# Token tile 3 last: samples and parameters ahead of it, parameter loads on two queues, an early ScalarE table load, and tile 3's squares on GpSimd

## What is computed

```
x = concat(x_prompt [512, 2048], x_sample [32, 2048])        # T = 544 tokens
xn = x * rsqrt(mean(x*x, axis=-1) + 1e-6) * norm_g           # RMSNorm over 2048
u  = xn @ ab_w_in                                            # first projection, 8 DeltaNet + 4 GLA heads
...                                                          # mixers, output projection, gate,
                                                             # second layer (SSD + RG-LRU), final norm
```

## Time and profile before

| what | value |
|---|---|
| median of 3 runs | 2451.35 us (2448.93 to 2452.26) |
| profiled execution, span from first to last instruction | 2447.1 us |
| median of the runs over that span | 4.25 us |
| TensorE busy | 2384.2 us, 97% |
| VectorE, ScalarE, GpSimd busy | 1280.8, 958.4, 373.5 us |
| mean granted TensorE clock | 0.993 |

### The profile page before, as it was taken

One profiled execution on the slowest core, in us unless ns is written; L12 is line 12 of the kernel. 1 busy time (PEld: TensorE's weight loads), 2 busy tenths in 40 slices (PEclk: granted clock), 3 DMA queues, 4 the chain that ended last, 5 costly groups with the idle time before them and its releaser, 6 DMA issues.

```text
span 2447.1 us, 50327 instructions
## 1 busy us (share of the span) xinstructions
PE 2384.2 (97%) x21567; PEld 2273.9 (93%) x21567; DVE 1280.8 (52%) x2387; ACT 958.4 (39%) x1547; POOL 373.5 (15%) x558
## 2 busy tenths in 40 slices
PE   7999999999999999999999999999999999999996
PEld 7998999988999999899999999988899999999996
DVE  6655656565654564622444465566656663243432
ACT  5523444323444344432332353443355553243332
POOL 3101101111101101111111212122212211111111
PEclk9999999999999999999999999999999999999998
DMA  9433333333344454552233343233323354223232
GB/s 232 115 103 107 116 98 116 108 90 106 108 121 117 136 152 122 194 161 87 87 97 109 110 114 92 70 89 87 86 80 103 95 190 127 87 83 96 79 88 76
DMA packets 375535, 271.16 MB, mean 111 GB/s; under 512 B 24419, under 2 KB 346733, under 8 KB 374800
## 3 DMA queue, kind: packets, MB, share of 16 engines
q1 hardware_dynamic: 341424, 172.53, 26.0%
q0 software_dynamic: 22080, 72.77, 9.3%
q10 hardware_dynamic: 11808, 22.63, 2.6%
HBM read 220.24 MB, written 48.37 MB: 110 GB/s over the span
## 4 chain that ended last, share of the span: by engine, by line
PE 86%; DVE 6%; ACT 5%; issue 2%; DMA 1%; POOL 0%; ACTq 0%; DVEq 0%; POOLq 0%
PE psd L582 71%; PE psw L605 2%; PE psw L604 2%; PE psw L632 1%; PE psw L682 1%; DVE arena L1967 1%; PE psw L660 1%; PE psw L668 1%; ACT w_hi L1136 1%; DVE w_lo L1683 1%; PE psw L674 0%; PE psw L646 0%; PE psw L654 0%; PE psw L971 0%; PE psw L1066 0%
## 5 line engine op out<-in xcount | busy, mean ns | idle before, releaser
L582 PE MATMUL psd<-xh,w_hi 128*128 128x272 f32 x5056 | 1098.3, 298 | 8.9 <-DVE w_lo L1683 5.3
L582 PE MATMUL psd<-xl,w_hi 128*128 128x272 f32 x5056 | 1048.4, 289 | 2.9 <-DVE xl L1745 2.1
L582 PE MATMUL psd<-xh,w_lo 128*128 128x272 f32 x5056 | 1045.2, 288 | 0.0
L582 PEld LDWEIGHTS psd<-xh,w_hi 128*128 128x128 f32 x5056 | 795.0, 189 | 60.0 <-issue 40.5
L582 PEld LDWEIGHTS psd<-xh,w_lo 128*128 128x128 f32 x5056 | 796.4, 189 | 0.0
L582 PEld LDWEIGHTS psd<-xl,w_hi 128*128 128x128 f32 x5056 | 792.2, 189 | 4.2 <-DVE xl L1745 3.1
L1683 DVE TENSOR_TENSOR w_lo<-w_raw,w_hi 128x512 fp32r<-128x512 f32 x632 | 433.7, 706 | 380.5 <-ACT w_hi L1136 379.4
L1136 ACT CAST w_hi<-w_raw 128x512 fp32r<-128x512 f32 x632 | 376.7, 616 | 573.2 <-PE psd L582 499.3
L2590 POOL TENSOR_TENSOR states<-states,extra 128x544 f32<-128x544 f32 x59 | 86.7, 1469 | 514.4 <-ACT extra L1191 514.3
L2377 DVE TENSOR_TENSOR extra<-psd,rstd 128x544 f32<-128x544 f32 x32 | 23.2, 724 | 156.0 <-PE psd L582 138.9
L2350 DVE TENSOR_TENSOR arena<-arena,psd 128x544 f32<-128x544 f32 x32 | 23.1, 721 | 136.7 <-PE psd L582 129.9
(11 more groups left out here) (514 smaller groups left out, 2376.9 us busy)
## 6 DMA issues: line engine op xcount, KB each, us to landing
w_raw<-in_ab_w_in_dram SPq DMA_DIRECT2D x224, 256.0 KB, 3.0
w_raw<-in_cd_w_in_dram SPq DMA_DIRECT2D x148, 256.0 KB, 3.0
w_raw<-in_ple_w_gate_dram SPq DMA_DIRECT2D x128, 256.0 KB, 3.1
w_raw<-in_ab_w_out_dram SPq DMA_DIRECT2D x64, 256.0 KB, 2.8
w_raw<-in_cd_w_out_dram SPq DMA_DIRECT2D x64, 256.0 KB, 2.8
uT_scratch<-mix ACTq DMA_DIRECT2D x53, 272.0 KB, 2.2
hT_scratch<-arena POOLq DMA_DIRECT2D x8, 1088.0 KB, 6.4
arena<-hT_scratch POOLq DMA_DIRECT2D x8, 1088.0 KB, 9.5
```

The costliest lines, as they stand in the source:

```text
L582: mm = pe.matmul(out[:, D0 + HALF * half:D0 + HALF * (half + 1)], w[:, r, k % QH, :], x[:, k, HALF * half:HALF * (half + 1)], start=(k == ...
```

## The change

The samples are loaded, transposed and copied between x1 and x2, and their copy to `arena` moves from ScalarE to VectorE, which counts up a new semaphore `smp_copied`. The `pv` group moves ahead of x3. Eight of the 15 parameter loads move from GpSimd's queue to ScalarE's, behind the load of the identity; on GpSimd the remaining seven come ahead of the clearing of `hist`. ScalarE runs a one-element copy before the first real one. VectorE no longer sums the squares of x3: GpSimd multiplies x3 by itself from `arena` and adds the 16 feature slices pairwise into `rstd[:, 384:512]`. `norm(0)` moves from behind slice 14 to behind slice 16, and waits for two counts of `sq_added`, the second from GpSimd.

```diff
+X_ORDER = (0, 1, NT, 2, 3)
...
-            for t in range(NT + 1):
+            for t in X_ORDER:
                 load_x(t)
...
             def norm(i):
                 W = group(("norm", i), "n")
-                pe.wait_ge(S["sq_added"], i + 1)
+                pe.wait_ge(S["sq_added"], i + 2 if i else 1)
                 if i == 0:
                     pe.matmul(W[:, SEQ - CUT:SEQ], ones[:, :], rstd[:, 0:CUT], start=True, stop=True)
+                    pe.wait_ge(S["sq_added"], 2)
...
-            for t in range(NT + 1):
+            for t in X_ORDER:
                 _, n = tok(t)
-                if t == NT:
+                if t == NT - 1:
                     W = group(u, "pv")
-                    pe.wait_ge(S["params_loaded"], 16 * len(PARAM_ROWS))
+                    pe.wait_ge(S["params_act"], 16 * PARAMS_ACT)
+                    pe.wait_ge(S["params_loaded"], 16 * (len(PARAM_ROWS) - PARAMS_ACT))
...
-            fill(KT - 2)
+            fill(SL)
             norm(0)
...
             act.dma_start(ident[:, :], I["cf"]).then_inc(S["consts_loaded"], 16)
+            for name, (col, row, n) in list(PARAM_ROWS.items())[:PARAMS_ACT]:
+                act.dma_start(cols[row:row + n, col, :], as_rows(I[name])).then_inc(S["params_act"], 16)
             act.wait_ge(S["dve_chain"], 1)
             act.wait_ge(S["pool_chain"], 1)
+            act.copy(small[0:1, 42:43], cst[0:1, 1:2])
...
-            for t in range(NT):
+            u = ("setup", 0)
+            for t in range(NT - 1):
+                if t == 2:
+                    for i in range(2):
+                        W = group(u, f"x{NT}{i}")
+                        dst = arena[:, :].rearrange("p (c t) -> p c t", c=KT)[:, 8 * i:8 * i + 8, SEQ:T]
+                        dve.tensor_copy(dst, W[:, :].rearrange("p (c t) -> p c t", c=8)[:, :, 0:NS])\
+                           .then_inc(S["smp_copied"], 1)
                 dve.wait_ge(S[f"xy_loaded{t}"], 16 * len(x_parts(t)))
...
-                    go(dve.tensor_tensor(tiles4(rstd[:, 0:SEQ]), bc4(ident[:, :]),
-                                         small[:, 20:24].unsqueeze(2).broadcast_to([P, NT, P]), ALU.mult))
+                    go(dve.tensor_tensor(rstd[:, 0:3 * P].rearrange("p (t n) -> p t n", t=3),
+                                         ident[:, :].unsqueeze(1).broadcast_to([P, 3, P]),
+                                         small[:, 20:23].unsqueeze(2).broadcast_to([P, 3, P]), ALU.mult))
...
             for q in range(3):
                 store_h(q)
+            x3 = arena3[:, :, 3 * P:SEQ]
+            sq3 = extra[:, 0:KT * P]
+            link(pool.tensor_tensor(sq3.rearrange("p (c t) -> p c t", c=KT), x3, x3, ALU.mult))
+            for n in (8 * P, 4 * P, 2 * P):
+                link(pool.tensor_tensor(sq3[:, 0:n], sq3[:, 0:n], sq3[:, n:2 * n], ALU.add))
             pool.wait_ge(S["sq_added"], 1)
+            pool.tensor_tensor(rstd[:, 3 * P:SEQ], sq3[:, 0:P], sq3[:, P:2 * P], ALU.add).then_inc(S["sq_added"], 1)
+            pool.wait_ge(S["sq_added"], 2)
```

More of the change, by code:

```diff
@@ L126, in once @@
         add(unit, name, reader, count[reader])
-    for t in range(NT + 1):
-        if t == NT:
+    for t in X_ORDER:
+        if t == NT - 1:
             once(("setup", 0), "pv", "in_copied")
         for i in range(2):
-            once(("setup", 0), f"x{t}{i}", "in_copied")
+            once(("setup", 0), f"x{t}{i}", "in_copied" if t < NT else "smp_copied")
     once(("norm", 0), "n", "nrm_ln")
@@ L183 @@
 SEMS = """w_landed0 w_landed1 w_landed2 w_landed3 w_landed4 w_landed5 hi_ready lo_ready slice_done dense_read0 dense_read1 stage_stored0 stage_stored1
-act_chain dve_chain pool_chain work_ready in_copied nrm_sq nrm_ln nrm_rstd x_hi x_ready y_done h_loaded0 h_loaded1 h_loaded2 h_loaded3 z_loaded dn_z gl_z cd_z x_read sq_added sq_summed
+act_chain dve_chain pool_chain work_ready in_copied nrm_sq nrm_ln nrm_rstd x_hi x_ready y_done h_loaded0 h_loaded1 h_loaded2 h_loaded3 z_loaded dn_z gl_z cd_z x_read sq_added sq_summed smp_copied params_act
 consts_loaded params_loaded rows_loaded xy_loaded0 xy_loaded1 xy_loaded2 xy_loaded3 xy_loaded4 xy_loaded5 h_stored
@@ L202 @@
     "lru_ba": (2, 100, 8), "lru_bx": (2, 108, 8), "lru_lambda": (2, 116, 8)}
-PARAM_DMAS = len(PARAM_ROWS) + 7
+PARAMS_ACT = 8
+PARAM_DMAS = len(PARAM_ROWS) - PARAMS_ACT + 7
 ROW_DMAS = 7
@@ L310, in trunk @@
         X_DMAS = [len(x_parts(t)) for t in range(NT + 1)] + [0]
-        X_COPIED = 2 * (NT + 1) + 1
+        X_COPIED = 2 * NT + 1
         def conv_rows(i):
@@ L1580, in _ @@
             act.dma_start(ident[:, :], I["cf"]).then_inc(S["consts_loaded"], 16)
+            for name, (col, row, n) in list(PARAM_ROWS.items())[:PARAMS_ACT]:
+                act.dma_start(cols[row:row + n, col, :], as_rows(I[name])).then_inc(S["params_act"], 16)
             act.wait_ge(S["dve_chain"], 1)
             act.wait_ge(S["pool_chain"], 1)
+            act.copy(small[0:1, 42:43], cst[0:1, 1:2])
             u = ("setup", 0)
-            for t in range(NT + 1):
+            for t in range(NT):
                 c0, n = tok(t)
-                if t == NT:
+                if t == NT - 1:
                     W = group(u, "pv")
@@ L1596, in _ @@
             act.wait_ge(S["in_copied"], X_COPIED)
+            act.wait_ge(S["smp_copied"], 2)
             for c in range(KT):
@@ L1610, in _ @@
             W = group(u, "h0")
+            act.wait_ge(S["pool_chain"], 2)
             act.copy(hist[:, 0:24, 0:24], W[:, 0:768].rearrange("p (i r) -> p i r", i=24)[:, :, 0:24]).then_inc(S["in_copied"], 1)
@@ L2548, in _ @@
             pool.memset(selp[:, :].bitcast(F32), 0.0)
-            pool.memset(small[:, :], 0.0)
+            link(pool.memset(small[:, :], 0.0))
+            for name, (col, row, n) in list(PARAM_ROWS.items())[PARAMS_ACT:]:
+                pool.dma_start(cols[row:row + n, col, :], as_rows(I[name])).then_inc(S["params_loaded"], 16)
             link(pool.memset(hist[:, :, :], 0.0))
-            for name, (col, row, n) in PARAM_ROWS.items():
-                pool.dma_start(cols[row:row + n, col, :], as_rows(I[name])).then_inc(S["params_loaded"], 16)
             pool.wait_ge(S["in_copied"], X_COPIED)
+            pool.wait_ge(S["smp_copied"], 2)
             arena3 = arena[:, :].rearrange("p (c t) -> p c t", c=KT)
```

## The result

The changed kernel takes 2459.46 us (median of 7 runs, 2457.85 to 2462.5) beside 2451.55 us for the kernel before (7 runs, 2446.91 to 2456.88): a ratio of 1.0031, with a 95% interval of 1.0022 to 1.0040. The medians differ by 7.9 us. The profiled execution's span is 2456.5 us against 2447.1 before; the mean granted clock is 0.991 against 0.993. Between 56 and 2400 us each of the two executions has two stretches of low clock, worth the same, so the clock is not where the time went.

The account below looks back on a forecast made before the run. VectorE paces the first output tile, and the chain through `cb` sets TensorE's resumption. Head -0.5, `rstd` -0.17, hold +7.5 and fifth operation +1.05 sum to +7.9: 2459.2 us from 2451.35, range 2454.0 to 2463.0.

Parts of the forecast that it names:

- the hold: In the first tile, GpSimd's squares of x3 stop VectorE's unbroken chain for their whole length: +7.5 us.
- the two rivals: VectorE held only in part, 2456.7 us, chance 0.08; or GpSimd's sums hide, 2451.3 us, chance 0.10.
- The head: At the program's start, without the table load, the samples' copies end earlier: -0.5 us, bounds 0 and 1.9.
- The fifth operation: GpSimd's 128x128 addition behind `sq_added`, ahead of its loads, waits for VectorE's running `xl`: +1.05 us.
- The transfer of `cb`: Load of the masks before TensorE resumes, 7.15 us before; could take less if moved to a quieter moment.
- The norm behind slice 16: ScalarE gets the norm 1.4 us later; TensorE's new stand of 0.8 at slice 20 is hidden, costing nothing.
- the resumption: TensorE's restart at slice 28, at 52.78 us before, expected near 60.7; only moving it was to matter.
- The clock: Rival: TensorE's low clock lasts into the second tile or returns after 60 us, costing 1.5 to 3; chance 0.10.

Follow-up runs that it names:

- the first experiment: The changed kernel with the four square sums of x3 back on VectorE and no squares on GpSimd: 2452.41 us, ratio 1.0010.
- the first two experiments: The changed kernel with x3's squares back on VectorE, norm behind slice 16 (2452.41 us), and the same with the norm behind slice 14 (2449.91 us).

## Why the prediction was right, point by point

**Its main step, the hold.** Right: GpSimd's time came back on VectorE, 8.15 us of it where the same squares take 8.08 alone. The products with an unread result (+7.29 in the chain), the memsets of equal length (0), the single product (+4.45) and the squares held back (0) leave no room for the two rivals. By the rule of the Trainium skill that the prediction weighed (SBUF — State Buffer, "Who interferes with whom"), `xl` is held as `w_lo` is; the trace agrees, with an `xl` of 5.22. That the one that starts first holds the port, the records don't show here: the held `xl` started at 22.44, GpSimd's product at 23.45. The size was 8.15 where I had 7.5. The product was mis-sized: it holds VectorE for 4.45 (by the single product), not 3.62. That leaves 3.70 for the three sums, where I had 3.94 and they take 4.48 alone, so they were not paid in full.

**The head.** I had -0.5, the profile shows -1.14, and the first dense matmul at 21.92 is outside the 22.2 to 22.8 that I had named. Here one profile is a poor judge. The first dense matmul was at 23.05, 22.72 and 21.11 in three profiled kernels with the old order (mean 22.29) and between 21.36 and 22.79 in nine with the new one (mean 21.76). The difference of the means is the 0.5 I had put down, but with spreads of 1.9 and 1.4 inside the groups, three and nine profiles can't tell it from nothing. What spreads them is how long x1's 16 transposes take: 3.67 and 3.64 in the two late old ones, 2.01 in the early one; 1.94 to 3.10 in the new ones, the longest of them in the two latest (3.07 for 22.33, 3.10 for 22.79).

**The fifth operation.** +1.01 where I had 1.05. It started at 45.46 and took 0.86 beside VectorE, 0.45 alone.

**The transfer of `cb`.** -0.47 where I had 0; named as a way for the size to be off.

**The norm behind slice 16.** The stand at slice 20 came as worked out, 0.82 for 0.8, and was hidden. But the step "TensorE does the same work in another order and has no new stand there" was incomplete. I followed the later norm result through the next two weight parts and stopped at the resumption; the third effect is 30 us further on. The weight parts converted after the norm free their raw buffers later (the first of their `w_lo` at 52.69, 8.5 after the earlier trace rows), the transfers of the parts six places on are issued and land later (conversions +8.9 and +9.6 against TensorE's +7.4), and the rows unit's 0.5 us of margin is used up. That makes a stand of 1.72 in the changed kernel, 3.56 in the first experiment (with about 1.7 of it the clock's), 1.10 with the norm's place alone and none where the squares are held back and the second conversion is less late than TensorE. That the norm's place is the cause is shown by the pair of the first two experiments; that it acts through the buffers is read from the traces and was not tested by itself.

**The clock.** The case in which it costs another 1.5 to 3 did not come about in the changed kernel: there is one stretch at 1.2 GHz near 66, as before near 61, and one more late, as before. In the kernel with the GpSimd squares alone there are three stretches more than before.

**The total.** The forecast was +7.9 at the resumption and +7.9 in the end. Measured: +7.43 and, with the stand that I missed, +9.15 in the spans. Up to the resumption the errors cancel: the hold 0.65 more, the head 0.64 and the transfer 0.47 less. The missed stand of 1.72 then leaves the spans 1.25 above the forecast. That the medians differ by 7.9 all the same is luck: the execution profiled before was a fast one (2.6 below its median), the one after less so (1.1).

## What to carry to other kernels

Work that is moved from a VectorE without gaps to GpSimd, with inputs in SBUF, can come back to VectorE at about its full length (here 8.15 us for squares that take 8.08), and the slower engine's time is the one that counts. This is shown for operations with two inputs in SBUF on both engines. Look first for a stretch where VectorE itself is idle, since x3's squares fit free of charge into its wait for the first weight part. A result that comes 1.4 us later must be followed through the buffers that it frees, down to the next place with a thin margin, not only to the next wait. Where the last link of the path is a load, ask what keeps it from being issued earlier; here that, together with a shorter chain, gave the only kernel whose interval lies below 1 (0.9989), by little.

## What the runs showed of the hardware that was not expected

- One GpSimd product of 3.62 us held VectorE for 4.45. The held `xl` (5.22) began about 1.0 us before the product's recorded start, in the changed kernel at about 22.4 against 23.45, and ended 0.6 after its end. Three stores had been issued by GpSimd just ahead of it. The same three stores stand ahead of the memsets, where no `xl` was held. What holds VectorE in that first microsecond is open.
- GpSimd writing alone, 7.44 us of memsets, held nothing: the chain was 16.15 with and without.
- At the start of the program, the same 16 transposes took between 2.01 and 3.67 us in different executions with the same program ahead of them, and with it the first dense matmul moves by up to 1.9 us (21.11 and 23.05). The rows give a granted clock of 1.00 from 8 to 20 us for both of these executions, so they don't tell the two rates apart; what sets them is open.
